# Attention in a two-layer encoder step: the score matmuls of the tile after next are issued ahead of the transposes of the current tile's weights

## The chip, the cores and the metric

The kernel runs on one core of one Trainium2 chip. The metric is device time in microseconds (us) of one execution, the median of several runs. Engines are named as the profile names them: PE is TensorE (matrix products; PEld is its weight load), ACT is ScalarE, DVE is VectorE, POOL is GpSimd, SP is SyncE.

## The reference, cut to what matters

The program is one step of a two-layer encoder: layer 0 is a gated DeltaNet with a convolutional FFN, layer 1 is multi-head latent attention with another convolutional FFN. The change lies in the attention of layer 1 alone. There are 8 heads; 1024 prompt positions attend among themselves, causally in chunks of 64, and 32 sample positions attend to 256 cached and 32 new positions.

```python
kv_up = (ckv_all @ p['kv_w_up']).reshape(B, past + L, MLA_HEADS, MLA_NOPE + MLA_V)
k_nope, v_all = kv_up[..., :MLA_NOPE], kv_up[..., MLA_NOPE:]
q = rms_norm(hin @ p['mla_w_dq'][j], p['mla_q_norm_g'][j]) @ p['mla_w_uq'][j]
...
s = jnp.einsum('bqhn,bkhn->bhqk', qn, k_nope) + jnp.einsum('bqhr,bkr->bhqk', qp, k_pe)
s = s.astype(jnp.float32) * MLA_SCALE
allowed = k_chunk[None, :] <= (qpos // CHUNK)[:, None]
p = jax.nn.softmax(jnp.where(allowed, s, -jnp.inf), axis=-1).astype(v.dtype)
return jnp.einsum('bhqk,bkhv->bqhv', p, v)
```

## The kernel before

Each engine has its own instruction list, written out by hand, and semaphores (`need`, `past`, `wait_ge`, `then_inc`) order the lists against each other. An engine works through its list in order: an instruction that waits holds up everything behind it on that engine.

**Tiles.** Attention is a loop over `x` from 0 to 71: `h, t = divmod(x, NQ)` with `NQ = 9`. Tiles t = 0 to 7 are 128 query rows each, with 128·(t+1) keys; tile t = 8 is the 32 sample rows with 288 keys. So tile t has t+1 key blocks of 128 (tile 8: two of 128 and one of 32).

**What PE does for a tile.** `pe_score` (L2603, matmuls L2615 to L2619) makes the scores: five products for each 512 keys or part of it, into PSUM banks 2·(x%2) and the next. `pe_weights` (L2622, L2630) transposes the normalised weights `PR`, one key block at a time, into bank 4 (blocks 0 to 3) and bank 5 (the rest). `pe_ov` (L2636, L2646) multiplies the transposed weights, copied to `PT`, by the values `VT`; on PE it issues two passes for each block. Between them stand the projections of the next head: `pe_k` (L2582) in tiles 0 to 3 and `pe_q` (L2594) in tiles 4, 6 and 8 of heads 0 to 6, both of them by `three` (L375, L378, L379). Tiles 5 and 7 have none, and the last head (h = 7) has none at all. In tile 0 of head 4 the values of the second half of the heads are also made (`pe_v`).

**What the others do.** For each x, ACT runs `act_pt(x)` (L2708: copies bank 4 to `PT`; it waits for the transposes of the first four blocks, and for the previous `pe_ov`), `act_normalise(x+1)` (L2706), `act_exp(x+2)` (L2698, needs the maximum of the scores), some splits of the next head's operands, and `act_ov(x)` (L2726). DVE runs `vec_normalise(x+1)` (a reciprocal, L2817), in tiles 4 to 7 the copy of bank 5 to `PT` (L2832), `vec_top(x+2)` (the row maximum of the scores, L2809 and L2811), and the casts of the next head's keys and queries. POOL makes the lower halves of split operands, SP loads weights.

**The waits around the change.** `pe_score(x+2)` waits until `act_exp(x)` has read the banks that it will write. `pe_weights(x)` waits for `act_normalise(x)`, and for the copies of tile x-1 out of banks 4 and 5. `pe_ov(x)` waits for both copies of tile x. The order on PE within one tile is the body of the loop in `pe_heads` (L2649).

Of the kernel before, what the change touches and what calls it, by code (L numbers as in the profile page):

```python
# [109 lines left out]
def build(nc, xT, cT, cB, ws, wada0, wada, par, cst, s0, cs, msk, pckv, pkpe, y, o_gdn, o_gcv, s_gdn, o_fcv, o_ckv, o_kpe):  # L110
# [4 lines left out]
    with ctx:  # L115
# [833 lines left out]
        def con(m, P=128, M=128):  # L949
            return CST[0:P, m, 0:M]  # L950
# [18 lines left out]
        def past(e, s, count):  # L969

            if count > 0:
                e.wait_ge(s, count)
# [1535 lines left out]
        def nbig(x):  # L2508

            h, t = divmod(x, NQ)  # L2510
            return len(BIG) * h + len([z for z in BIG if z < t])

        def key_blocks(t):

            q0, P, k0, nk = QTILES[t]
            first = 0 if t < GT else GT
            return [(first + m, min(128, nk - 128 * m)) for m in range(-(-nk // 128))]
# [11 lines left out]
        def q_chunk(t):  # L2529

            return 0 if t < 2 else 1 if t < 5 else 2
# [27 lines left out]
        def evacuated(e, p):  # L2559

            e.wait_ge(v_ev if p[0] == "v" else kq_ev, P_EV[p])

        def pe_v(e, B, b):
            p = ("v", B, b)
            w, c0 = slab_v(B) % 2, V_TILES[b]
            if b == 0:
                all_here(e, (hi_done, slab_v(B) + 1), (lo_done, slab_v(B) + 1))
            if P_PREV[p]:
                evacuated(e, P_PREV[p])
            if (B, b) == (1, 1):  # L2570
                past(e, ov_ev, NQ * HALF)
            out = PS[:, P_BANK[p], :]
            for k in range(LB):
                c = slice(512 * k, 512 * k + 512)
                mm = e.matmul(out, CKH[:, k, c0:c0 + 128], WH[w][:, c], start=(k == 0), stop=False)
                if b == 0 and k == 0:
                    mm.then_inc(ws_begun, 1)
                e.matmul(out, CKH[:, k, c0:c0 + 128], WL[w][:, c], start=False, stop=False)
                mm = e.matmul(out, CKL[:, k, c0:c0 + 128], WH[w][:, c], start=False, stop=(k == LB - 1))
            mm.then_inc(pj_ps, 1)  # L2580

        def pe_k(e, h, ch):  # L2582
            p = ("k", h, ch)
            n, (c0, cw) = slab_h(h), KCH[ch]
            if ch == 0:
                all_here(e, (hi_done, n + 1), (lo_done, n + 1))
            if P_PREV[p]:
                evacuated(e, P_PREV[p])
            for k in range(LB):
                mm = three(e, PS[:, P_BANK[p], 0:cw], n % 2, 128 * (QB + k), CKH[:, k, c0:c0 + cw], CKL[:, k, c0:c0 + cw], k == 0, k == LB - 1,  # L2590
                           ch == 0 and k == 0)
            mm.then_inc(pj_ps, 1)

        def pe_q(e, h, ch):  # L2594
            p = ("q", h, ch)
            n, (c0, cw) = slab_h(h), CHS[ch]
            if P_PREV[p]:
                evacuated(e, P_PREV[p])
            for k in range(QB):
                mm = three(e, PS[:, P_BANK[p], 0:cw], n % 2, 128 * k, QLH[:, k, c0:c0 + cw], QLL[:, k, c0:c0 + cw], k == 0, k == QB - 1)  # L2600
            mm.then_inc(pj_ps, 1)

        def pe_score(e, x):  # L2603
            h, t = divmod(x, NQ)
            q0, P, k0, nk = QTILES[t]
            past(e, ex_rdy, x - 1)
            evacuated(e, ("q", h, q_chunk(t)))
            evacuated(e, ("k", h, len(KCH) - 1))
            e.wait_ge(qc_rdy, 3 * h + q_chunk(t) + 1)
            e.wait_ge(kp_rdy, half_count(h, q_chunk(t)))  # L2610
            for s0_ in range(0, nk, 512):
                w_ = min(512, nk - s0_)
                out = PS[0:P, 2 * (x % 2) + s0_ // 512, 0:w_]
                kc = slice(k0 + s0_, k0 + s0_ + w_)
                e.matmul(out, QTH[:, q0:q0 + P], KTH[h % 2][:, kc], start=True, stop=False)  # L2615
                e.matmul(out, QTH[:, q0:q0 + P], KTL[h % 2][:, kc], start=False, stop=False)
                e.matmul(out, QTL[:, q0:q0 + P], KTH[h % 2][:, kc], start=False, stop=False)
                e.matmul(out, QPHH[:, q0:q0 + P], KPHL[:, kc], start=False, stop=False)
                mm = e.matmul(out, QPLM[:, q0:q0 + P], KPHM[:, kc], start=False, stop=True)  # L2619
            mm.then_inc(sc_ps, 1)  # L2620

        def pe_weights(e, x):  # L2622
            t = x % NQ
            q0, P, k0, nk = QTILES[t]
            e.wait_ge(nm_rdy, x + 1)
            past(e, pt_ev, x)
            past(e, pu_ev, nbig(x))
            blocks = key_blocks(t)
            for m, (b, kw) in enumerate(blocks):
                mm = e.transpose(PS[0:kw, 4 + m // 4, (m % 4) * 128:(m % 4) * 128 + P], PR[x % 2][0:P, 128 * m:128 * m + kw], con(C_ID, P, P))  # L2630
                if m == min(4, len(blocks)) - 1:
                    mm.then_inc(pt_ps, 1)
            if t in BIG:
                mm.then_inc(pu_ps, 1)

        def pe_ov(e, x):  # L2636
            h, t = divmod(x, NQ)
            P = QTILES[t][1]
            evacuated(e, ("v", h // HALF, NV - 1))
            e.wait_ge(pt_ev, x + 1)  # L2640
            past(e, pu_ev, nbig(x + 1))
            past(e, ov_ev, x)
            blocks = key_blocks(t)
            c = 128 * (h % HALF)
            for m, (b, kw) in enumerate(blocks):
                mm = e.matmul(PS[:, 6, 0:P], VT[0:kw, b, c:c + 128], PT[0:kw, m, 0:P], start=(m == 0), stop=(m == len(blocks) - 1))  # L2646
            mm.then_inc(ov_ps, 1)

        def pe_heads(e):  # L2649
            e.wait_ge(rot_ev, 15)  # L2650
            e.wait_ge(kp_rdy, 5)

            def free(banks):
                for p in P_FIRST[-6:]:
                    if P_BANK[p] in banks:
                        evacuated(e, p)
            free((0, 1))
            pe_score(e, 0)
            free((2, 3))
            pe_score(e, 1)  # L2660
            free((4, 5))
            for x in range(NX):
                h, t = divmod(x, NQ)
                pe_weights(e, x)
                if x + 2 < NX:
                    pe_score(e, x + 2)
                if (h, t) == (HALF, 0):
                    for b in range(NV):
                        pe_v(e, 1, b)
                if h + 1 < HEADS and t < len(KCH):  # L2670
                    pe_k(e, h + 1, t)
                if h + 1 < HEADS and t in Q_AT:
                    pe_q(e, h + 1, Q_AT[t])
                pe_ov(e, x)

        def half_count(h, ch):

            return 5 + 6 * h + 2 * (ch + 1)
# [193 lines left out]
        def pe_rest(e):  # L2872
# [53 lines left out]
            for ch in range(NCH):  # L2926
                pe_q(e, 0, ch)
            pe_heads(e)
            e.wait_ge(ov_ev, NX)

# [692 lines left out]
```

## Time and profile before

| | |
|---|---|
| median of 3 runs | 2988.99 us (2988.23 to 2992.25) |
| the profiled execution: its time | 2989.8 us |
| its span, first to last instruction | 2987.8 us |
| PE busy | 2892.0 us (97%), weight loads 2776.2 us (93%) |
| DVE busy | 2230.5 us (75%) |
| ACT busy | 1269.8 us (42%) |
| POOL busy | 1096.9 us (37%) |
| mean granted clock of PE | 0.990 of full speed |
| attention's tile loop, all 8 heads | from about 1815.6 to 2100.8 us of the span |

The tile loop is a tenth of the span. Times of day in the rows below are microseconds from the start of the span. A matmul's record overlaps its neighbours', since matmuls are pipelined: the distance between two starts is what one of them costs.

### The profile page before, as it was taken

The numbers are of one execution on the slowest core, as the hardware profiler recorded it, in microseconds if no ns is written. First come the engines' busy times: TensorE is split into PE (matmuls) and PEld (weight loads), VectorE is DVE, ScalarE is ACT, GpSimd is POOL, SyncE is SP. The second block draws the span as 40 slices with busy tenths as digits, with TensorE's granted clock in tenths as the row PEclk, the third lists the DMA queues.
The fourth block names the chain that finished last, engine by engine and source line by source line (L and its number), as shares of the span: only waits on it lengthen the run. The fifth ranks groups of instructions, "written<-read, shape, count | busy, mean of one in ns | idle before, by whom it ended". The sixth has DMA issues, their size and how long they took to land.

```text
span 2987.8 us, 52051 instructions
## 1 busy us (share of the span) xinstructions
PE 2892.0 (97%) x18516; PEld 2776.2 (93%) x18516; DVE 2230.5 (75%) x3363; ACT 1269.8 (42%) x2433; POOL 1096.9 (37%) x726
## 2 busy tenths in 40 slices
PE   6999989999999999999999999999999999999997
PEld 5999986999998999999999788989989999999996
DVE  7999985777728888877888865544368788788787
ACT  4333334555416533333332755666255233333324
POOL 2333444666331434443334222111214333344332
PEclk9999998999999999999999999999999999999999
DMA  7455654211111111111111030102201111111111
GB/s 281 163 175 177 210 190 179 62 52 49 37 43 36 43 50 49 43 51 54 42 49 51 29 125 30 37 30 80 80 29 50 50 49 49 42 49 49 49 49 60
DMA packets 87018, 225.75 MB, mean 76 GB/s; under 512 B 9436, under 2 KB 41124, under 8 KB 85860
## 3 DMA queue, kind: packets, MB, share of 16 engines
q1 hardware_dynamic: 47812, 142.24, 14.1%
q10 hardware_dynamic: 39072, 81.72, 8.0%
q8 instruction: 85, 1.39, 0.2%
q14 instruction: 49, 0.40, 0.0%
HBM read 192.59 MB, written 31.35 MB: 75 GB/s over the span
## 4 chain that ended last, share of the span: by engine, by line
PE 77%; DVE 10%; issue 5%; ACT 3%; DMA 2%; ACTq 1%; POOL 0%; SPq 0%; DVEq 0%; POOLq 0%
PE PS L375 14%; PE PS L378 13%; PE PS L379 13%; PE PS L1754 6%; PE PS L1758 6%; PE PS L1757 6%; DVE CV L3423 4%; PE PS L999 3%; PE PS L2646 2%; PE PS L1015 2%; PE PS L505 2%; DVE PS L879 1%; PE PS L2630 1%; PE PS L1071 1%; ACT CV L3263 1%
## 5 line engine op out<-in xcount | busy, mean ns | idle before, releaser
L371 POOL TENSOR_TENSOR WL<-RAW,WH 128x1024 fp32r<-128x1024 f32 x192 | 502.3, 2616 | 1022.1 <-ACT WH L366 1022.0
L375 PE MATMUL PS<-HH,WH 128*128 128x352 f32 x2120 | 698.4, 329 | 35.0 <-issue 16.0
L379 PE MATMUL PS<-HH,WL 128*128 128x352 f32 x2120 | 685.3, 323 | 0.0
L378 PE MATMUL PS<-HL,WH 128*128 128x352 f32 x2120 | 684.8, 323 | 0.0
L375 PEld LDWEIGHTS PS<-HH,WH 128*128 128x128 f32 x2120 | 401.3, 189 | 53.4 <-issue 43.3
L366 ACT ACTIVATE WH<-RAW 128x1024 fp32r<-128x1024 f32 x199 | 210.4, 1057 | 456.3 <-PE PS L375 355.2
L378 PEld LDWEIGHTS PS<-HL,WH 128*128 128x128 f32 x2120 | 402.4, 190 | 1.5
L379 PEld LDWEIGHTS PS<-HH,WL 128*128 128x128 f32 x2120 | 401.8, 190 | 0.0
L2173 DVE SCALAR_TENSOR_TENSOR X<-PS,ADA,X 128x352 f32<-128x352 f32 (+1 forms) x704 | 319.2, 485 | 84.8 <-PE PS L379 80.4
L379 PE MATMUL PS<-FH,WL 128*128 128x352 f32 x960 | 310.7, 324 | 0.0
L375 PE MATMUL PS<-FH,WH 128*128 128x352 f32 x960 | 310.4, 323 | 0.0
L378 PE MATMUL PS<-FL,WH 128*128 128x352 f32 x960 | 310.3, 323 | 0.0
L2145 DVE SCALAR_TENSOR_TENSOR CF<-UF,PSF,CF 128x1060 f32<-128x1060 f32 x176 | 289.2, 1697 | 0.0
L879 DVE CUSTOM_DVE_ANT_0 PS<-ADR,CB 128x1024 f32<-128x1024 f32 x144 | 196.4, 1364 | 6.4 <-DMA ADR<-wada 1.9
L375 PEld LDWEIGHTS PS<-FH,WH 128*128 128x128 f32 x960 | 180.6, 188 | 0.3
L378 PEld LDWEIGHTS PS<-FL,WH 128*128 128x128 f32 x960 | 180.5, 188 | 0.0
L379 PEld LDWEIGHTS PS<-FH,WL 128*128 128x128 f32 x960 | 180.0, 187 | 0.0
L1576 POOL TENSOR_TENSOR AM<-M,CST 128x1024 f32<-128x1024 f32 (+1 forms) x61 | 135.6, 2240 | 60.6 <-PE PS L999 50.1
L3423 DVE SCALAR_TENSOR_TENSOR CV<-U,PST,CV 128x1060 f32<-128x1060 f32 x72 | 139.8, 1942 | 17.0 <-ACT CV L3263 15.3
L1754 PE MATMUL PS<-HH,WH 128*128 128x352 f32 x456 | 147.3, 323 | 0.0
L1758 PE MATMUL PS<-HH,WL 128*128 128x352 f32 x456 | 146.8, 322 | 0.0
L1757 PE MATMUL PS<-HL,WH 128*128 128x352 f32 x456 | 146.6, 321 | 0.0
(395 smaller groups left out, 6280.1 us busy)
## 6 DMA issues: line engine op xcount, KB each, us to landing
RAW<-ws SPq DMA_DIRECT2D x199, 512.0 KB, 3.3
ADR<-wada ACTq DMA_DIRECT2D x66, 512.0 KB, 4.8
scr<-V ACTq DMA_DIRECT2D x32, 528.0 KB, 3.0
X<-xT SPq DMA_DIRECT2D x3, 1408.0 KB, 20.7
OUTT<-scr SPq DMA_DIRECT2D x1, 4224.0 KB, 15.5
y<-X SPq DMA_DIRECT2D x6, 704.0 KB, 4.8
AD0R<-wada SPq DMA_DIRECT2D x8, 512.0 KB, 13.1
AD<-wada SPq DMA_DIRECT2D x2, 2048.0 KB, 14.9
```

The costliest lines, as they stand in the source:

```text
L366: e.activation(WH[u][:, :], RAW[:, u, :], ACT.Copy).then_inc(hi_done, 1)
L371: e.tensor_tensor(WL[u][:, :], RAW[:, u, :], WH[u][:, :].bitcast(fp32), ALU.subtract).then_inc(lo_done, 1)
L375: mm = e.matmul(out, WH[w][:, c:c + 128], mh, start=first, stop=False)
L378: e.matmul(out, WH[w][:, c:c + 128], ml, start=False, stop=False)
L379: return e.matmul(out, WL[w][:, c:c + 128], mh, start=False, stop=last)
L879: ins = v.tensor_tensor_reduce(out=PS[:, B_ADA:B_ADA + 2, :].rearrange("p b c -> p (b c)"), in0=ADR[:, 3 * u + q, :], in1=CB[:, st, :], sc ...
L1754: mm = e.matmul(out, lhs, xh[:, r + k, c0:c0 + CW], start=first and k == 0, stop=False, skip_group_check=not first)
L1757: e.matmul(out, lhs, xl[:, r + k, c0:c0 + CW], start=False, stop=False, skip_group_check=not first)
L1758: mm = e.matmul(out, wl[:, c + 128 * k:c + 128 * k + 128], xh[:, r + k, c0:c0 + CW], start=False, stop=k == 3, skip_group_check=not first)
L2145: ins = v.scalar_tensor_tensor(CF[:, half, :], src, w, CF[:, half, :], ALU.mult, ALU.add)
L2173: ins = v.scalar_tensor_tensor(X[:, m, a:a + w], PS[:, bank_(k), a - c0:a - c0 + w], ADA[:, s, 2 * KB + m, st:st + 1], X[:, m, a:a + w], A ...
L3423: v.scalar_tensor_tensor(CV[u][:, :], src(j), PST[:, u, j:j + 1], CV[u][:, :], ALU.mult, ALU.add)\
```

## The change

In the loop of `pe_heads` the call that issues the scores of tile x+2 moves ahead of the call that issues the transposes of tile x. Nothing else is touched.

```diff
             for x in range(NX):
                 h, t = divmod(x, NQ)
-                pe_weights(e, x)
                 if x + 2 < NX:
                     pe_score(e, x + 2)
+                pe_weights(e, x)
                 if (h, t) == (HALF, 0):
                     for b in range(NV):
                         pe_v(e, 1, b)
```

The instruction lists of DVE and ACT are the same in both kernels, and PE has the same instructions in another order. In the rows of the two lists below, `PR_235` and `PR_236` are the two buffers of weights, `CST` the identity matrix, `KTH`/`KTL` and `QTH`/`QTL` the upper and lower halves of keys and queries, `KPHL`, `KPHM`, `QPHH`, `QPLM` the rotary parts; x6 means one for each of six key blocks.

PE in tile 5 of head 0, before: the transposes of six blocks, the scores of tile 7 (two times five products), then the product with the values.

```order
L2630 MATMUL PS<-CST,PR_236 128x128 x6
L2615 MATMUL PS<-KTH_233,QTH 128x512
L2616 MATMUL PS<-KTL_245,QTH 128x512
L2617 MATMUL PS<-KTH_233,QTL 128x512
L2618 MATMUL PS<-KPHL,QPHH 128x512
L2619 MATMUL PS<-KPHM,QPLM 128x512
L2615 MATMUL PS<-KTH_233,QTH 128x512
L2616 MATMUL PS<-KTL_245,QTH 128x512
L2617 MATMUL PS<-KTH_233,QTL 128x512
L2618 MATMUL PS<-KPHL,QPHH 128x512
L2619 MATMUL PS<-KPHM,QPLM 128x512
L2646 MATMUL PS<-PT,VT 128x128 x6
```

The same place in the changed kernel:

```order
L2615 MATMUL PS<-KTH_233,QTH 128x512
L2616 MATMUL PS<-KTL_245,QTH 128x512
L2617 MATMUL PS<-KTH_233,QTL 128x512
L2618 MATMUL PS<-KPHL,QPHH 128x512
L2619 MATMUL PS<-KPHM,QPLM 128x512
L2615 MATMUL PS<-KTH_233,QTH 128x512
L2616 MATMUL PS<-KTL_245,QTH 128x512
L2617 MATMUL PS<-KTH_233,QTL 128x512
L2618 MATMUL PS<-KPHL,QPHH 128x512
L2619 MATMUL PS<-KPHM,QPLM 128x512
L2630 MATMUL PS<-CST,PR_236 128x128 x6
L2646 MATMUL PS<-PT,VT 128x128 x6
```

The ten score matmuls stood between the transposes and the product that reads the transposed weights; now nothing stands between those two.

PE in tile 7 of head 0, before (the score group here belongs to tile 0 of head 1):

```order
L2630 MATMUL PS<-CST,PR_236 128x128 x8
L2615 MATMUL PS<-KTH_234,QTH 128x128
L2616 MATMUL PS<-KTL_246,QTH 128x128
L2617 MATMUL PS<-KTH_234,QTL 128x128
L2618 MATMUL PS<-KPHL,QPHH 128x128
L2619 MATMUL PS<-KPHM,QPLM 128x128
L2646 MATMUL PS<-PT,VT 128x128 x8
```

The same place in the changed kernel:

```order
L2615 MATMUL PS<-KTH_234,QTH 128x128
L2616 MATMUL PS<-KTL_246,QTH 128x128
L2617 MATMUL PS<-KTH_234,QTL 128x128
L2618 MATMUL PS<-KPHL,QPHH 128x128
L2619 MATMUL PS<-KPHM,QPLM 128x128
L2630 MATMUL PS<-CST,PR_236 128x128 x8
L2646 MATMUL PS<-PT,VT 128x128 x8
```

The eight transposes moved from ahead of the five short score matmuls to behind them, directly before the product with the values.

## Rows read from the trace of the kernel before

**Rows 1.** The page's engine line: busy us (share of the span) xinstructions.

```profile
PE 2892.0 (97%) x18516; PEld 2776.2 (93%) x18516; DVE 2230.5 (75%) x3363; ACT 1269.8 (42%) x2433; POOL 1096.9 (37%) x726
```

**Rows 2.** Windows: us, PE, PEld, DVE, ACT, POOL busy, PEclk, DMA share, GB/s.

```profile
1851.90:1885.40 33.50, 32.97 (x234) 31.23 (x234) 17.59 (x45) 22.42 (x53) 5.20 (x4) 1.00 0.09 33
...
2090.00:2096.00 6.00, 4.89 (x42) 4.30 (x40) 2.29 (x8) 4.16 (x10) 0.00 (x0) 1.00 0.01 3
```

**Rows 3.** Waits, 1817 to 2102: engine line waited for: us in total, times, longest.

```profile
DVE SMX L2809 <- PE PS L2619: 76.9, 56, 2.4
ACT PR L2698 <- DVE SMX L2811: 67.3, 63, 1.9
...
PE PS L2646 <- DVE PT L2832: 5.7, 9, 1.0
...
PE PS L2630 <- ACT PR L2706: 1.7, 1, 1.7
```

**Rows 4.** Timeline, tile 7 of head 1: start us, us, engine, line, operation, [idle before].

```profile
1881.35 1.04 PE L2630 MATMUL PS<-CST,PR 128*128 128x128 f32 x8
...
1881.99 0.60 ACT L2715 ACTIVATE PT<-PS 128x512 f32<-128x512 f32 x1 [0.16 <-PE PS L2630]
1882.14 0.30 PE L2615 MATMUL PS<-KTH,QTH 128*128 128x128 f32 x1
...
1882.48 0.69 DVE L2832 COPY PT<-PS 128x512 f32<-128x512 f32 x1 [1.35 <-PE PS L2630]
...
1882.62 0.27 PE L2619 MATMUL PS<-KPHM,QPLM 128*128 128x128 f32 x1
...
1883.42 2.02 PE L2646 MATMUL PS<-PT,VT 128*128 128x128 f32 x16 [0.53 <-DVE PT L2832]
```

**Rows 5.** Timeline, tile 5 of head 1.

```profile
1872.61 0.82 PE L2630 MATMUL PS<-CST,PR 128*128 128x128 f32 x6
...
1873.18 0.48 PE L2615 MATMUL PS<-KTH,QTH 128*128 128x512 f32 x1
...
1873.52 0.42 DVE L2832 COPY PT<-PS 128x256 f32<-128x256 f32 x1 [0.67 <-PE PS L2630]
```

**Rows 6.** Timeline, tile 3 of head 1: transposes, first key projection, product with values.

```profile
1863.68 0.60 PE L2630 MATMUL PS<-CST,PR 128*128 128x128 f32 x4
...
1865.87 0.28 PE L375 MATMUL PS<-CKH,WH 128*128 128x256 f32 x1
...
1866.58 1.05 PE L2646 MATMUL PS<-PT,VT 128*128 128x128 f32 x8
```

**Rows 7.** Timelines of PE and ACT, last head: tiles 6 and 8.

```profile
2093.20 1.80 PE L2646 MATMUL PS<-PT,VT 128*128 128x128 f32 x14 [0.97 <-DVE PT L2832]
...
2099.62 0.94 PE L2646 MATMUL PS<-PT,VT 128*128 128x32 f32 x6 [0.43 <-ACT PT L2717]
...
2099.35 0.17 ACT L2717 ACTIVATE PT<-PS 32x32 f32<-32x32 f32 x1
```

**Rows 8.** Groups by shape on ACT, tile loop: count | busy us, mean ns | idle before.

```profile
L2715 ACT ACTIVATE PT<-PS 128x512 f32<-128x512 f32 x40 | 23.9, 597 | 0.9 <-PE PS L2630 0.6
...
L2715 ACT ACTIVATE PT<-PS 128x128 f32<-128x128 f32 x8 | 2.2, 278 | 3.9 <-ACT OH L2726 3.3 <-PE PS L2630 0.6
```

**Rows 9.** Groups by shape on DVE, then ACT: row maximum and exponential of tile 7.

```profile
L2809 DVE TENSOR_REDUCE SMX<-PS 128x1 f32<-128x1024 f32 x8 | 9.8, 1224 | 13.8 <-PE PS L2619 13.8
...
L2698 ACT ACTIVATE PR<-PS,SMX 128x1024 f32<-128x1024 f32 x8 | 8.9, 1117 | 14.0 <-DVE SMX L2811 14.0
```

**Rows 10.** Timeline, tile 0 of head 0, the loop's first tile.

```profile
1819.67 0.30 PE L2630 MATMUL PS<-CST,PR 128*128 128x128 f32 x1 [1.68 <-ACT PR L2706]
...
1823.14 0.63 PE L2646 MATMUL PS<-PT,VT 128*128 128x128 f32 x2
```

**Rows 11.** Windows in the loop's first tile (columns as in rows 2).

```profile
1821.00:1822.00 1.00, 1.00 (x5) 1.00 (x5) 0.31 (x1) 0.00 (x0) 0.00 (x0) 0.50 0.00 0
1822.00:1823.50 1.50, 1.50 (x7) 1.50 (x7) 0.52 (x3) 0.67 (x2) 0.00 (x0) 0.50 0.00 0
```

## The prediction

> **What bounds the kernel now.** I read the engine line of the page first [rows 1]: PE is busy 97% of the span, its weight loads 93%, no other engine over 75%. So the question is only what the change does to PE's own time. Next the windows of the attention loop: one whole head, the second, takes 33.5 us, and PE is busy for 32.97 of them at the full granted clock, while DVE is busy for 17.6 and ACT for 22.4 [rows 2]. PE bounds the loop too, and it has no more than about half a microsecond a head to give back.
>
> Then the waits of the loop [rows 3]. DVE waits 76.9 us for scores and ACT 67.3 us for the row maximum: the reader may think that the softmax chain starves, but these engines have slack, and PE hardly waits for them. PE waits once for normalised weights (1.7 us, the first tile) and 9 times for DVE's copy of transposed weights (5.7 us in all). The wait that PE meets is thus not "scores come too late" but "the copy of the transposed weights is not out yet". What the change moves is the work that covers that copy.
>
> **The latency that has to be covered.** From the start of a tile's transposes to the start of its product with the values, PE needs: the transposes, the copies out of PSUM, and the way back.
> - Tile 7 [rows 4]: the transposes start at 1881.35; ACT's copy of the first four blocks starts 0.64 later and lasts 0.60; DVE's copy of the others starts 1.13 after the start, lasts 0.69, and PE goes on 0.25 after it ends. In all 2.07 us. Eight transposes last 1.04 as a row, the last alone about 0.27, so each takes 0.11 to issue and eight take 0.88.
> - Tile 5 [rows 5]: DVE's copy starts 0.91 after the transposes, lasts 0.42; with the same 0.25 that is 1.58 us.
> - Where ACT's copy ends last, PE follows it by 0.10 (2099.52 to 2099.62 [rows 7]). So tile 3 needs 0.64 + 0.60 + 0.10 = 1.34. For three, two and one blocks the copy begins 0.11 earlier for each block fewer and lasts between 0.60 and 0.28 [rows 8]; with 0.49 and 0.39 between these ends that gives 1.12 (tile 2), 0.92 (tile 1) and 0.69 (tile 0). Tile 4: its five blocks need 1.34 on both paths. Tile 6: 1.02 + 0.56 + 0.25 = 1.83, with the copy of three blocks between those of two and four.
>
> **The change part by part.** No instruction is added or removed, and no DMA is moved; DVE's, ACT's, POOL's and SP's lists stand as they were. On PE the scores of tile x+2 go from behind the transposes of tile x to ahead of them.
>
> *(a) Their own cost: nothing.* Same instructions. Ahead of them stands a wait for the exponential of tile x; it used to be met by the transposes' own wait for the normalised weights, which come after that exponential on ACT. Its heaviest place is tile 7, whose maximum and exponential last 1.22 and 1.12 us [rows 9]. Counted from the start of tile 5's transposes, DVE's copy ends at 1.33, the maximum at 2.6, the exponential at about 4. PE asks for it after the product of tile 5 (1.58 to 2.9), the scores of tile 8 (about 0.7), the transposes of tile 6 (0.77), a projection (1.45) and a product (14 passes at 0.11): at about 7.3. Behind this wait on PE stand the transposes; they don't get later.
>
> *(b) The cover that is gone, heads 0 to 6.* In tiles 0, 1, 2, 4, 6 and 8 projections still stand between transposes and product. A key projection of 256 columns is 0.71 long (1865.87 to 1866.58, six matmuls [rows 6]), so one of 352 columns 0.97 and a query projection, nine matmuls, 1.45. Transposes plus projection are then 1.08, 1.19 and 1.30 in tiles 0 to 2 against 0.69, 0.92 and 1.12 needed; 2.0 or more against 1.34 and 1.83 in tiles 4 and 6; tile 8 is short and has 1.45 behind it. These six cost nothing, and what hides the copies is the projection alone. Three tiles are left:
>  - tile 3: 0.44 + 0.71 = 1.15 against 1.34, so 0.2 is exposed;
>  - tile 5: nothing but 0.66 of transposes against 1.58, so 0.92;
>  - tile 7: already exposed before (0.53 idle), because five short matmuls did not cover it. They start at 1882.14 and the last at 1882.62 [rows 4]; at 0.12 apart they are 0.6 long. The 2.07 stay, and the 0.6 is added in front.
>  That is 1.7 us a head, for seven heads **12.0 us**.
>
> *(c) The last head.* No projection stands anywhere. Exposed are, by the latencies above less 0.11 a block, 0.58, 0.70, 0.79, 0.90, 0.79, 0.92 and 1.06 in tiles 0 to 6, together 5.7; tiles 7 and 8 have no score group before or after and stay. From it goes what was idle before: 0.97 in tile 6 [rows 7], and in tile 0 a little that I leave out: 5.7 - 1.0, **4.7 us**. Tile 6's idle time was late for another reason (DVE's copy stood behind the reciprocal of tile 7), and with scores earlier that goes; the plain copy latency takes its place.
>
> *(d) The first tile, the one gain.* PE waited 1.68 us before its first transposes at 1819.67, and then ran at half clock, 0.50 in both windows [rows 11]; the product started at 1823.14 [rows 10], 3.47 later. Now the third score group (0.9 us at full clock) fits into that wait. If the clock then stays up, transposes and key projection take 0.11 + 0.97, and the product starts at 1820.75: **2.4 us less**. If the clock falls all the same, the projection takes twice as long and 1.4 is left; none is the other bound.
>
> *(e) A stall that moves.* Where the copy in tiles 4 to 7 comes after the transposes, the row maximum of tile x+2 stands behind it on DVE although its scores are there. For tile 7 that is the chain of (a): its weights, normalised about 2 us after the exponential, are asked for at about 8. Nobody waits for it.
>
> **Sum:** 12.0 + 4.7 - 2.4 = **+14.3 us**. The profiled execution took 2989.8 us with a span of 2987.8, so such an execution would take 3004.1; the median of the runs is 0.8 lower, 2989.0, and gives **3003.3 us**.
>
> **Bounds.** Tile 3 may cost nothing (if the way back is shorter) or 0.5 (if ACT's copy comes late behind the weight split that ACT makes in tile 2); tile 5 from 0.80 to 1.05; tile 7 from 0.5 to 0.7. That is 1.3 to 2.25 a head, 9.1 to 15.8 for seven. The last head 3.5 to 5.2, the first tile -2.4 to 0. Ends: +10.2 and +21.0, or 2999.2 and 3010.0. I take the middle of each, since each is read from the same place of this loop.
>
> **The rivals.**
> *Faster: the softmax chain was what PE waited for.* With the scores issued first, the maximum, the exponential and the normalisation of tile x+2 start earlier by the length of the transposes; if PE's idle time hangs on that chain, it goes. Its place is the wait of the transposes for normalised weights, and it decides once that wait is met in every head. For it speaks the first tile, and tile 6 of the last head. Price: at most the 1.7 and 5.7 of [rows 3] and the lost clock of the first tile, under 2 us: some -9, or 2980. Against it: in 72 tiles PE met that wait once, and 8 of the 9 other waits are for the copy itself, which can't begin sooner. The Trainium skill (Perfetto Trace Analysis, Optimization Strategy) advises just this: find what blocks the bound engine and make those dependencies start sooner. By that rule the change should help; by the rows it starts sooner a chain that isn't blocking, and delays the start of one that is.
>
> *Slower by more: the clock falls.* With a gap of about 1 us every three or four in the last head, or in tiles 5 and 7 of each head, the granted clock might drop to half as it did in the first tile. There it was at 0.50 for at least the 2.5 us of the two windows [rows 11], so a fall costs some 1.3 to 1.7 us; two falls in the last head give 3006, one more in each of the seven heads 3017. Against it: between 2090 and 2096 PE was busy for 4.89 of 6 us, with the gap of 0.97 in it, and the clock stayed at 1.00 [rows 2, 7]. The Trainium skill (TensorE: Matmul & The Clock Gate, A second HAM failure mode) tells of a kernel whose clock swung between its levels because PE idled briefly between groups of matmuls; the rows just named show such a gap without it.
>
> *No change within 0.2%.* Copies could be hidden if PE were not the bound, or if the gaps were given back behind the loop: PE waits for ACT's splits after the last tile anyhow. But these start only with the last product, so the delay passes through. +3, or 2992, would need exposures a fifth of those above.
>
> **How the numbers follow.** About 0.2% (6 us) is what a measurement here can tell from no change; +10.2 is beyond it. The forecast with its bounds gets 0.82, the clock rival 0.08 (a third of it inside the range), faster 0.05, no change 0.05. The range is the forecast's own bounds, 2999 to 3010; left out are the two last and most of the clock rival, about 0.15. Slower is 0.82 + 0.08 = 0.90, same 0.05, faster 0.05.
>
> **What would show it.** In the changed profile: PE's wait for DVE's copy (L2646 <- L2832) over 15 times and over 10 us; waits of L2646 for ACT's copy (L2715), which did not exist, in tile 3 and all over the last head, some 5 us; windows of one head at about 35.2 us with PE still busy for 33; the last head longer by 4 to 5; no half clock near 1821. The prediction is wrong if a head's window stays at 33.5 (the copies are hidden by something I missed), if PE's waits for PR appear, or if the clock reads under 1.00 within the loop.

## The result, and the profile after

The changed kernel takes 3005.5 us (median of 5 runs, 3004.3 to 3006.44) against 2988.99 us (5 runs, two more than in the table before, 2985.85 to 2992.25): a ratio of 1.0051, 95% interval 1.004 to 1.0061, so it is slower by 0.5%. The forecast was 3003.3 us, range 2999 to 3010. The profiled execution has a span of 3002.3 us, 14.5 more than the 2987.8 of before; the sum had said 14.3.

The page's engine line of the changed kernel, to be read against [rows 1]:

```profile
PE 2896.1 (96%) x18516; PEld 2775.3 (92%) x18516; DVE 2229.6 (74%) x3363; ACT 1270.2 (42%) x2433; POOL 1097.2 (37%) x726
```

The work is the same; PE is idle for longer. The waits from 1815 to 2118, against [rows 3] (engine line waited for: us in total, times, longest):

```profile
ACT PT L2715 <- PE PS L2630: 73.8, 71, 2.0
DVE PT L2832 <- PE PS L2630: 57.7, 32, 2.7
DVE SMX L2809 <- PE PS L2619: 40.5, 39, 1.9
...
PE PS L2646 <- DVE PT L2832: 15.4, 17, 1.0
...
ACT PR L2698 <- DVE SMX L2811: 10.3, 25, 0.6
...
PE PS L2646 <- issue: 2.3, 4, 0.7
...
PE PS L2646 <- ACT PT L2715: 0.6, 1, 0.6
```

The earlier scores do what one would want on the softmax side: DVE's wait for scores falls from 76.9 to 40.5 us, ACT's for the maximum from 67.3 to 10.3. Both engines now wait at another place, for the transposes (ACT 73.8 us, before 1.2; DVE 57.7, before 15.6), since these come later in the tile. None of that is PE's time. PE's wait for DVE's copy grows from 5.7 us in 9 tiles to 15.4 in 17, and new waits of the product for ACT's copy appear, of which the profile names one as such and puts four to "issue".

Windows of the changed kernel: the end of the first tile, one whole head, and the last head (columns as in [rows 2]).

```profile
1821.00:1822.00 1.00, 1.00 (x7) 0.87 (x6) 0.82 (x2) 0.66 (x3) 0.00 (x0) 1.00 0.00 0
1822.00:1823.50 1.50, 1.50 (x11) 1.37 (x10) 1.15 (x4) 0.75 (x2) 0.00 (x0) 1.00 0.00 0
1855.30:1890.70 35.40, 33.56 (x234) 31.15 (x233) 17.47 (x45) 22.35 (x53) 5.19 (x4) 1.00 0.09 31
2090.00:2100.00 10.00, 8.05 (x54) 7.20 (x55) 3.56 (x9) 6.11 (x13) 0.00 (x0) 1.00 0.24 96
2100.00:2115.00 15.00, 11.86 (x88) 10.39 (x87) 3.93 (x10) 7.82 (x18) 0.00 (x0) 1.00 0.00 1
```

A head takes 35.4 us instead of 33.5 [rows 2]. The windows from 1821 to 1823.5 read 1.00 where they read 0.50 [rows 11]. In the last head PE is busy for only 80% of the time, with a gap in nearly every tile, and the clock stays at 1.00.

Tiles 5 and 7 of head 1 in the timeline of the changed kernel, the same places as [rows 5] and [rows 4]:

```profile
1874.54 0.82 PE L2630 MATMUL PS<-CST,PR 128*128 128x128 f32 x6
...
1875.17 0.60 ACT L2715 ACTIVATE PT<-PS 128x512 f32<-128x512 f32 x1 [1.45 <-PE PS L2630]
...
1875.45 0.42 DVE L2832 COPY PT<-PS 128x256 f32<-128x256 f32 x1 [2.74 <-PE PS L2630]
...
1875.79 1.21 DVE L2809 TENSOR_REDUCE SMX<-PS 128x1 f32<-128x1024 f32 x1
...
1876.13 1.58 PE L2646 MATMUL PS<-PT,VT 128*128 128x128 f32 x12 [0.77 <-DVE PT L2832]
...
1878.23 0.20 ACT L2698 ACTIVATION_READ_ACCUMULATOR PR<-PS,SMX 128x1 f32 x1
...
1881.91 0.30 PE L2615 MATMUL PS<-KTH,QTH 128*128 128x128 f32 x1
...
1882.50 1.06 PE L2630 MATMUL PS<-CST,PR 128*128 128x128 f32 x8
...
1883.65 0.69 DVE L2832 COPY PT<-PS 128x512 f32<-128x512 f32 x1 [1.88 <-PE PS L2630]
...
1884.60 2.02 PE L2646 MATMUL PS<-PT,VT 128*128 128x128 f32 x16 [1.04 <-DVE PT L2832]
```

From transposes to product it is 1.59 us in tile 5 (1874.54 to 1876.13) and 2.10 in tile 7 (1882.50 to 1884.60); the sum had 1.58 and 2.07. Tile 7's maximum stands behind DVE's copy in tile 5 as expected, and its exponential is read out by 1878.4, 3.5 us before PE asks for it at 1881.91.

From one product's start to the next, in head 2 (both profiled executions, worked out from the starts of the L2646 rows):

| tile | 0 | 1 | 2 | 3 | 4 | 5 | 6 | 7 | 8 | head |
|---|---|---|---|---|---|---|---|---|---|---|
| before, us | 2.80 | 2.56 | 3.47 | 3.55 | 4.97 | 4.07 | 4.20 | 3.63 | 4.36 | 33.61 |
| after, us | 2.84 | 2.56 | 3.42 | 3.75 | 4.99 | 5.00 | 4.28 | 4.16 | 4.36 | 35.36 |

The last head in the timeline of PE, after the change (tiles 1, 3, 4, 5, 6):

```profile
2087.25 0.68 PE L2646 MATMUL PS<-PT,VT 128*128 128x128 f32 x4 [0.52 <-issue]
...
2094.40 1.13 PE L2646 MATMUL PS<-PT,VT 128*128 128x128 f32 x8 [0.73 <-issue]
...
2098.74 1.35 PE L2646 MATMUL PS<-PT,VT 128*128 128x128 f32 x10 [0.64 <-ACT PT L2715]
...
2103.84 1.57 PE L2646 MATMUL PS<-PT,VT 128*128 128x128 f32 x12 [0.77 <-DVE PT L2832]
...
2107.74 0.46 PE L2646 MATMUL PS<-PT,VT 128*128 128x128 f32 x2 [0.90 <-DVE PT L2832]
```

The distances from transposes to product are 0.69, 0.90, 1.13, 1.33, 1.34, 1.59 and 1.83 us in tiles 0 to 6, where the sum had 0.69, 0.92, 1.12, 1.34, 1.34, 1.58 and 1.83.

To tell where the time of a run went, I use one measure below: the **loop**, from the first score matmul to the product of the last tile, in the profiled execution. It is 284.00 us before (1815.62 to 2099.62) and 298.31 after, +14.3. It is steadier than a run's time: another execution with before's loop order had its loop begin 6.8 us later, and it still took 283.97 (it is one of the experiments below).

### The profile page after: what moved, and what is told of

It reads as the page before. It is cut to its first block, busy times and chain, and to the rows that moved or that the text cites. A ratio compares the mean times of both kernels' runs of the same rounds, so it can differ in the third digit from the quotient of the medians.

```text
span 3002.3 us, 52051 instructions
## 1 busy us (share of the span) xinstructions
PE 2896.1 (96%) x18516; PEld 2775.3 (92%) x18516; DVE 2229.6 (74%) x3363; ACT 1270.2 (42%) x2433; POOL 1097.2 (37%) x726
## 4 chain that ended last, share of the span: by engine, by line
PE 77%; DVE 11%; issue 6%; ACT 4%; DMA 1%; ACTq 1%; POOL 0%; SPq 0%; DVEq 0%; POOLq 0%
PE PS L375 13%; PE PS L379 13%; PE PS L378 13%; PE PS L1754 6%; PE PS L1758 6%; PE PS L1757 6%; DVE CV L3423 4%; PE PS L999 3%; PE PS L2646 3%; PE PS L1015 2%; PE PS L505 2%; DVE PS L879 1%; PE PS L2630 1%; PE PS L1071 1%; ACT CV L3263 1%
## 6 DMA issues: line engine op xcount, KB each, us to landing
OUTT<-scr SPq DMA_DIRECT2D x1, 4224.0 KB, 15.4
```

## The experiments

**Where the loss sits.** Three kernels move the scores in some tiles only. All three replace the two calls in `pe_heads` by

```diff
-                pe_weights(e, x)
-                if x + 2 < NX:
-                    pe_score(e, x + 2)
+                first = x == 0
+                if first and x + 2 < NX:
+                    pe_score(e, x + 2)
+                pe_weights(e, x)
+                if not first and x + 2 < NX:
+                    pe_score(e, x + 2)
```

and differ in the condition: `x == 0`, then `h + 1 < HEADS and t not in (5, 7)`, then `t == 5`. (Three added lines shift the line numbers behind them by 3.)

The first tile alone:

> Scores first in the loop's first tile alone (x = 0). Cover (my theory: all the loss is the copy of transposed weights with nothing beside it, and the one gain is the first tile): the first product with the values starts about 2.4 us earlier than in the kernel before, nothing else moves, span about 2985.4 against 2987.8. Softmax chain (rival: earlier scores help wherever PE waits): the same here. Clock (rival: the gain is only the clock that stays up): if the clock near 1821 still falls to half, the gain is about 1 us; if it stays, 2.4.

2987.86 us, ratio 0.9991 (0.9982 to 1.0): as a whole not to be told from no change. The loop shows it: 281.28 us, -2.7. From the first score to the first product it is 5.09 us instead of 7.52, and on to the second product 2.56 instead of 2.83, because the half clock of the kernel before reached into tile 1. Here the granted clock reads 1.00 from 1817 to 1825, so the rival's case of a clock that falls all the same did not come. Timeline of PE:

```profile
1820.32 0.33 PE L2630 MATMUL PS<-CST,PR 128*128 128x128 f32 x1 [0.20 <-ACT PR L2709]
...
1821.46 0.38 PE L2646 MATMUL PS<-PT,VT 128*128 128x128 f32 x2
```

The wait of 1.68 us [rows 10] is down to 0.20, and the product starts 1.14 after the transposes instead of 3.47.

Scores first where a projection covers the copy:

> Scores first wherever a projection still stands behind the transposes (tiles 0 to 4, 6 and 8 of heads 0 to 6), the old order in tiles 5 and 7 and in the whole last head. Cover: -2.4 for the first tile, +0.19 a head in tile 3 and +0.19 a head in tiles 4 and 6 (as the changed kernel showed), so +0.3 us, -1 to +1. Waits on exponentials (rival: what PE loses comes from the score group's own wait, now ahead of everything): most of the loss of the changed kernel stays, since most of the moved groups are moved here too: +8 us or more.

2990.31 us, ratio 0.9997 (0.9988 to 1.0006), and a loop of 283.44, -0.6. PE's wait for DVE's copy is 5.8 us in 9 tiles, as before. 49 of the 70 moved score groups are moved here, and most of the loss is gone. It is not quite nothing: against the run with the first tile alone the loop is 2.2 us longer, and 1.4 of that is tile 3, 0.20 in each of seven heads, where the projection does not cover the whole copy. So the group's own wait for an exponential costs 0.8 us at most in 49 tiles, and the loss is in the 21 others.

Tile 5 alone:

> Scores first in tile 5 of each head alone. Cover: +0.94 us in each of 8 heads, +7.5 us, as PE waits of about 0.8 us for DVE's copy of two blocks, and nothing in any other tile. Waits on exponentials: one moved group of nine, so a ninth of the changed kernel's loss, 2 us or less.

2998.16 us, ratio 1.0028 (1.0018 to 1.0038). The loop is 291.93, +7.9, or 1.0 for each of the 8 tiles. The clock fell in the first tile of this execution too, a little later than in the kernel before, and the second tile (from the first product on, 3.59 us against 2.83) had more of it:

```profile
1822.20:1823.20 1.00, 1.00 (x5) 0.95 (x5) 0.96 (x2) 0.42 (x2) 0.00 (x0) 0.50 0.00 0
```

From the first score to the second product both kernels take the same, 10.34 and 10.35, so none of the 7.9 is the clock. In head 2 tile 5 is 0.96 longer and tile 6 0.09. Eight groups out of 70 cost more than half of the whole loss.

**Is it the copy?** Here DVE copies bank 5 twice in tile 5, once in the changed kernel and once in the kernel before (the second copy waits for the first):

```diff
+                    if t == 5:
+                        v.tensor_copy(PT[:, 4:4 + nb, :], bank(5)[:, 0:nb, :]).then_inc(x_scaled, 1)
+                        v.wait_ge(x_scaled, 2 + KB + h + 1)
                     v.tensor_copy(PT[:, 4:4 + nb, :], bank(5)[:, 0:nb, :]).then_inc(pu_ev, 1)
```

> The changed kernel, with DVE's copy of bank 5 made twice in tile 5 (the same data, the second after the first). Cover: the copy is what PE waits for there, so tile 5 gets longer by the second copy, 0.42 and some 0.05 to 0.1 between them: +0.5 us in 8 heads, 4 us over the changed kernel, and its wait in tile 5 about 1.3 us. If PE waits for something else there, no change.

> The kernel before, with the same copy made twice in tile 5. Cover: from transposes to product it would need 2.1 us and has 2.96 with the ten score matmuls between, so nothing changes: within 0.5 us of the kernel before. If the copy's length matters by itself, +4 as in the changed kernel.

In the changed kernel: 3007.35 us, 1.0053 (1.0038 to 1.0069), loop 301.99, which is 3.7 over the changed kernel. Tile 5 of head 2 takes 5.47 instead of 5.00:

```profile
1910.69 0.81 PE L2630 MATMUL PS<-CST,PR 128*128 128x128 f32 x6
...
1911.60 0.42 DVE L2833 COPY PT<-PS 128x256 f32<-128x256 f32 x1 [2.71 <-PE PS L2630]
...
1912.05 0.42 DVE L2835 COPY PT<-PS 128x256 f32<-128x256 f32 x1
...
1912.74 1.46 PE L2646 MATMUL PS<-PT,VT 128*128 128x128 f32 x11 [1.24 <-DVE PT L2835]
```

In the kernel before the same second copy costs nothing: 2990.4 us, 1.0004 (0.9994 to 1.0014), loop 283.97 against 284.00. It ends at 1914.85, and the scores cover it until 1916.02:

```profile
1913.64 0.47 PE L2615 MATMUL PS<-KTH,QTH 128*128 128x512 f32 x1
...
1913.97 0.42 DVE L2833 COPY PT<-PS 128x256 f32<-128x256 f32 x1 [0.67 <-PE PS L2630]
...
1914.43 0.42 DVE L2835 COPY PT<-PS 128x256 f32<-128x256 f32 x1
...
1916.02 1.50 PE L2646 MATMUL PS<-PT,VT 128*128 128x128 f32 x12
```

This pair is the plainest evidence: the same work, on the path in one order and off it in the other.

**Cover from somewhere else.** The query projection of tile 8 is made in tile 7, which has none:

```diff
-        Q_AT, Q_USED = {4: 0, 6: 1, 8: 2}, (3, 6, 9)
+        Q_AT, Q_USED = {4: 0, 6: 1, 7: 2}, (3, 6, 9)
```

once in the changed kernel, once in the kernel before together with the scores first in the first tile.

> The changed kernel with the query projection of tile 8 moved to tile 7. Cover: in tile 7 the 2.07 us from transposes to product are now covered (0.88 + 1.45), which takes away the wait of 1.03 us; tile 8 loses its cover and waits about 0.45. Net -0.6 to -0.75 us a head in 7 heads: some 4.5 us faster than the changed kernel, about +10 over the kernel before; the waits of L2646 for DVE's copy fall from 17 to about 10. If something else than cover made the loss, the projection's place changes nothing: +14.5.

3000.49 us, 1.0041 (1.0026 to 1.0056); the loop is 292.78, 5.5 less than in the changed kernel (4.5 was expected). PE's wait for DVE's copy falls to 8.1 us in 10 tiles, and tile 8 has got a gap of 0.43.

> The kernel before with two edits: scores first in the first tile alone, and the query projection of tile 8 moved to tile 7. Cover: -2.4 for the first tile, and PE's idle 0.53 us in tile 7 of heads 0 to 6 goes (-3.7); tile 8 keeps its score group as cover (0.27 + 0.6 against 0.76). In all -6.1 us, a span of about 2981.7. If the waits of tile 7 are not a matter of cover, -2.4.

2983.41 us against 2990.04, ratio 0.9977 (0.9967 to 0.9986): faster than the kernel before by 0.2%, and than the changed kernel by more. The loop is 276.48, -7.5 (-6.1 was expected). PE in tiles 7 and 8 of head 2:

```profile
1910.94 1.04 PE L2630 MATMUL PS<-CST,PR 128*128 128x128 f32 x8
...
1911.74 0.30 PE L2615 MATMUL PS<-KTH,QTH 128*128 128x128 f32 x1
...
1913.82 1.95 PE L2646 MATMUL PS<-PT,VT 128*128 128x128 f32 x16
...
1915.70 0.34 PE L2630 MATMUL PS<-CST,PR 32*128 32x32 f32 x3
...
1916.66 0.86 PE L2646 MATMUL PS<-PT,VT 128*128 128x32 f32 x6
```

Neither product waits any more. Tiles 7 and 8 together take 7.28 us instead of 7.99, so 0.7 a head is won and not the 0.53 that the profile shows as idle.

**The other direction.** If scores may not go earlier, may they go later? They were put behind the projections, directly ahead of the product, and DVE made its casts ahead of the maximum:

```diff
                     pe_q(e, h + 1, Q_AT[t])
+                if x + 2 < NX and (h, t) != (HALF, 0):
+                    pe_score(e, x + 2)
                 pe_ov(e, x)
```

(the call behind `pe_weights` stays for tile 0 of head 4 alone; in `vec_heads` the call of `vec_top(v, x + 2)` goes behind those of `vec_k` and `vec_q`, but for the same tile).

> The opposite move: the scores of tile x+2 go behind the projections, directly ahead of the product with the values (but for tile 0 of head 4), and DVE casts the projections before it takes the maximum. Cover: the same work stands between transposes and product, so PE loses nothing: head windows of 33.5 us as before, time within 1 us of the kernel before. Softmax chain: every maximum and exponential in the 49 tiles with a projection starts 0.7 to 1.45 us later; if PE hangs on that chain, it waits for normalised weights (L2630 <- L2706), up to 50 us more in all, 10 us or more if only a fifth of it is felt.

Both expectations missed. 3008.39 us, 1.0057 (1.0042 to 1.0073), a loop of 298.75, +14.8. (The clock stayed at 1.00 in the first tile of this execution, which gives back 1.5 us up to the second product; the rest of the loop loses 16.3.) But PE waits for normalised weights in the first tile only (1.7 us, as in [rows 3]). What it waits for, 12.4 us in 20 tiles, is ACT's copy. Tile 0 of head 2 in the timeline:

```profile
1898.05 0.33 PE L2630 MATMUL PS<-CST,PR 128*128 128x128 f32 x1
...
1898.56 0.48 ACT L2700 ACTIVATE PR<-PS,SMX 128x256 f32<-128x256 f32 x1 [2.78 <-DVE SMX L2813]
...
1899.02 1.01 ACT L2686 ACTIVATE QPHH<-QPE 64x352 fp32r<-64x352 f32 x2
...
1900.05 0.20 ACT L2728 ACTIVATE OH<-PS 128x32 f32<-128x32 f32 x1
...
1900.73 0.28 ACT L2717 ACTIVATE PT<-PS 128x128 f32<-128x128 f32 x1 [0.48 <-ACT OH L2728]
...
1901.11 0.46 PE L2646 MATMUL PS<-PT,VT 128*128 128x128 f32 x2 [0.88 <-ACT PT L2717]
```

The transposes are done at 1898.4, but ACT copies them only at 1900.73. It had been idle for 2.78 us ahead of an exponential that needs the late maximum, and the rest of its list (the exponential, the halves of the next queries, the output of the tile before) then ran down late. The copy was not short of cover; it was queued behind a late instruction. On this I formed a second theory, and took the two edits apart.

> One half of the run with the scores last: PE's order is that of the kernel before, and only DVE makes its casts of a tile's projection before the maximum of tile x+2. The run with both edits lost 15 to 18 us without any wait of PE for normalised weights. Queue theory (formed on that run): a late maximum makes a late exponential, which stands on ACT ahead of the next tile's copy to PT, so PE waits for that copy (L2646 <- L2715). Here the maximum comes up to 2.1 us later in tiles 0 to 3 (the rest of the projection and 1.05 us of casts), so the same waits appear, +15 us or so, from +8 to +28. If instead the place of the scores on PE made that loss and DVE's order is harmless: within 2 us of the kernel before.

3034.43 us, 1.0151 (1.013 to 1.0173), loop 324.48, +40.5: more than the theory's +28, in its direction. The waits of the two engines:

```profile
ACT PR L2698 <- DVE SMX L2811: 114.3, 49, 4.3
...
PE PS L2646 <- ACT PT L2715: 34.4, 29, 2.6
```

PE's order is untouched here, and what stands between transposes and product is the same; the new order on DVE alone does it, and what PE waits for is again ACT's copy. Why it costs more than the +28 was not tried.

> The other half: PE's scores last as in that run, DVE's order as in the kernel before (maximum first, then the casts). Queue theory: the maximum is only as late as the scores, but the casts now wait behind it, and bank 7, which the next tile's projection writes, comes free late: PE waits for the casts (L375 <- L2793, L2802), an estimated 1.3 to 1.7 us in tiles 1 to 3 and 0.8 in tile 4 of seven heads, +20 to +40 us. If only the length of cover matters (transposes to product), within 1 us of the kernel before.

3041.98 us, 1.0176 (1.0154 to 1.0199), loop 334.38, +50.4, again above the expected +40. The waits:

```profile
PE PS L375 <- DVE KTL L2795: 30.6, 28, 1.8
...
PE PS L375 <- DVE QTL L2804: 4.6, 5, 0.9
```

Now the casts are late, bank 7 is not free, and the next projection waits for it. These two rows name 35 of the 50 us; what makes up the rest was not taken apart. So DVE's order in the run with both edits was the lesser evil: it took away these waits and left the queue on ACT.

## Why the prediction was right

The sum by parts, against the profiled executions:

| part | predicted | measured |
|---|---|---|
| first tile, first score to first product | -2.4 | -2.43 (7.52 to 5.09) |
| heads 0 to 6, first product to that of tile 8 of head 6 | +12.0 | +12.5 (249.00 to 261.48) |
| the last head, on to the last product | +4.7 | +4.3 (27.48 to 31.74) |
| loop | +14.3 | +14.3 |

That the loop agrees to 0.1 us is in part luck, since two misses cancel: the heads lost 0.5 more than the sum, and the last head 0.4 less. The mechanism and each part's size are what held.

*(a) The scores' own wait costs nothing.* Right within 0.8 us: that is what the run with 49 of the 70 groups moved leaves for it beside tile 3's copy. The times fit too: counted from the start of tile 5's transposes, tile 7's exponential is there after 3.9 us and PE asks for it after 7.4, where the prediction had 4 and 7.3.

*(b) The cover that is gone.* Right in place and size: in head 2, +0.20 in tile 3 (0.2 said), +0.93 in tile 5 (0.92), +0.53 in tile 7 (0.6), nothing in tiles 1 and 8. (The 12.5 of the table is 12.75 lost, less 0.27 won in tile 1 of head 0, for which see (d).) Small things remain that I did not foresee, +0.08 in tile 6 and up to 0.05 either way in tiles 0, 2 and 4; what makes them was not tried.

*(c) The last head.* The latencies were right to 0.02 us, the sum 0.4 too high. From product to product, tiles 0 and 1 lose 0.30 and 0.43 us where the sum had 0.58 and 0.70; the others are within 0.1. In both, PE waited already in the kernel before, which the sum took as nothing. In tile 0 the last score matmul starts at 2073.79, they stand 0.18 apart, and the product starts at 2074.29: 0.3 us of waiting, of which the profile shows 0.16 as idle. In tile 1 the transposes waited for the normalised weights, these two rows of the kernel before:

```profile
2074.22 0.51 ACT L2706 ACTIVATE PR<-PR,SMX 128x256 f32<-128x256 f32 x1
...
2074.78 0.44 PE L2630 MATMUL PS<-CST,PR 128*128 128x128 f32 x2
```

They start 0.49 us after the product of tile 0. In the changed kernel PE goes on after that product within 0.23, so 0.26 came back there.

*(d) The first tile.* Right, and the size was a little larger than the table's row says: the half clock of the kernel before reached into tile 1, so up to the second product the changed order takes 7.65 us against 10.35, 2.7 less. How the gain divides can be estimated. In the run with the scores last the same wait of 1.68 us stood ahead of the first transposes, PE had the same matmuls to do up to the first product, and the clock stayed at 1.00; that product came 6.09 us after the first score. Against the 5.09 of the changed order, 1.0 us is the group that fits into the wait. The other 1.7 (1.4 in the first tile) is the clock that no longer falls. It is not a matter of how late it falls: in two other executions with before's order at this place, tile 5 alone and the second copy in the kernel before, the first product came after 6.75 and 6.80 us, but the second after 10.34 in both. Had the clock stayed up in the execution that was read, the gain would have been 1.0 and the loop's loss about 16.

*(e) The maximum behind DVE's copy.* Right: nobody waited for it. But "nobody waits" has a limit that the text did not see: the two kernels with a later maximum show that its lateness reaches PE through ACT's queue, and not where I had looked, at the wait for normalised weights.

The rivals. The softmax chain was named as the faster case, and it fell: the chain's waits shrank by 93 us in all (36.4 on DVE, 57.0 on ACT), and what PE got of it beyond the first tile is the 0.26 us in tile 1 of the last head (see (c)). There the prediction was wrong in a detail: it counted one wait of PE for normalised weights in 72 tiles, by a row of waits that does not hold this second one. The Trainium skill (Perfetto Trace Analysis, Optimization Strategy) says to make the dependencies that block the bound engine start sooner. By that advice one must first ask which dependency blocks; the trace agrees with it in the first tile, where it was the softmax, and in the others it was the copy. The clock rival fell too: in the last head PE was busy for 8.05 of 10 and 11.86 of 15 us with a gap in most tiles, at 1.00 throughout. The brief idle times between groups that the Trainium skill warns of (TensorE: Matmul & The Clock Gate, A second HAM failure mode) did not lower it here.

Of the signs announced, the head's window, the waits for DVE's copy (17 times, 15.4 us) and the absent half clock came as said. The waits for ACT's copy were said to show as such in tile 3 and the last head, some 5 us; the profile names one, of 0.6 us, and calls four others "issue" (2.3 us), and tile 3's 0.2 shows in no wait at all, only in the distance between products. The median moved by 16.5 us and not 14.3, with the interval from 12 to 18; runs of one kernel lie up to 11 us apart (the kernel before, 26 runs, 2986.3 to 2997.7), and the loop's part is 14.3 in the profiled pair.

One statement at the start of the prediction was set too low: that PE has no more than about half a microsecond a head to give back. With the projection of tile 8 moved to tile 7, the kernel before gave back 0.7.

## What to carry to other kernels

On an in-order engine a block of work has two roles: its own result, and the cover that it gives to whatever the engine waits for next. Before moving it, take the latency from the producer to the consumer that it stood between (here transposes, copy and way back), and subtract the work that will still stand there; what is left of the latency, tile by tile, is the price. Starting a chain sooner gains only where the bound engine waits for that chain, and starting it later can hurt at an unexpected place, since a late instruction holds everything queued behind it on its own engine.

## What the runs showed of the hardware

The granted clock after one and the same pattern of waits is not the same in every execution. In six of the profiled executions PE was idle for 0.86 to 0.88 and then for 1.68 or 1.69 us ahead of the loop's first transposes. The clock then fell to 0.50 in five of them, the kernel before among them [rows 11], and stayed at 1.00 in one, the run with the scores last. The clearest pair is that run and the one with PE's scores last alone, since PE's instruction list is the same in both. First two windows of the one where it stayed, then one of the other:

```profile
1827.00:1829.00 2.00, 1.50 (x9) 1.53 (x10) 0.23 (x2) 1.03 (x4) 0.00 (x0) 1.00 0.00 0
1829.00:1831.00 2.00, 2.00 (x15) 1.83 (x14) 1.60 (x4) 0.30 (x1) 0.00 (x0) 1.00 0.00 0
```

```profile
1817.00:1819.00 2.00, 2.00 (x8) 2.00 (x8) 0.00 (x0) 0.10 (x1) 0.00 (x0) 0.50 0.00 0
```

What decides it is not shown here.

Idle time as the profile states it is not the whole of what a missing cover costs, because it is counted from the end of a matmul's record, and the next matmul could have started before that. In tile 7 before [rows 4] the last score matmul starts at 1882.62 and its record lasts 0.27 us, but these matmuls start 0.12 apart. From 1882.74, where the next one could start, to the product at 1883.42 it is 0.68 us; the profile shows 0.53 as idle, and giving the tile cover won 0.7 over tiles 7 and 8. The same holds for tile 3 of the changed kernel, where 0.2 us shows as no wait at all, and for the gaps of its last head, each some 0.16 us shorter than the exposure. The distance between two starts is the surer measure.
